# A 64-step recurrence scan with each head in its own 64-column tile, and its operands re-laid out in memory

## The chip, the cores and the metric

The kernel runs on one core of one Trainium2 chip. The metric is the device time of one execution in microseconds (us). Three runs of the kernel before gave 4600.29, 4602.82 and 4605.73 us; their median is 4602.82 us.

## What is computed

One transformer block on 512 tokens of width 2048: a projection of x by `w_in`, then two mixers side by side (stick-breaking attention and an RWKV7 time mix, 16 heads of 64 each), their gated sum, a layer norm, a mixture of 16384 rank-one experts, and a last layer norm. The change concerns the RWKV7 time mix:

```
def step(state, inp):                       # state: 16 heads of 64 x 64
    r_t, lw_t, k_t, v_t, a_t, b_t = inp
    sa = einsum('bhvk,bhk->bhv', state, a_t)
    state = (state * exp(lw_t)[:, :, None, :] + sa[..., None] * b_t[:, :, None, :]
             + v_t[..., None] * k_t[:, :, None, :])
    return state, einsum('bhvk,bhk->bhv', state, r_t)
```

Both kernels compute it in 8 chunks of 64 tokens (`NC = 8`, `L = 64`). Inside a chunk the recurrence is solved with a triangular 64 x 64 inverse for each head, so that a chunk is four matrix steps for each head: X (the state and the values seen through the rows a and k), U = inverse times X, S (the new state, from U, V and the decayed keys) and Y (the output). Only the state goes from one chunk to the next.

## The kernel before

The program is a row of stages with a barrier of all engines between them. Four of them matter here.

- `rwkv_prepare` (tensors `b_...`) goes over 8 blocks m of 128 channels (two heads, e = 0 and 1). Each block makes `ar` (rows a and r of all 8 chunks), `bk`, the masked products `gm` (in `b_wide`), the transposed keys `bkt` and the values `vt`, and SyncE (its queue is SPq in the rows) stores them to device memory for the scan: `stores(sp, m)`, lines 480 to 492, six DMAs a block. Beside this work TensorE multiplies pieces of late columns of `w_in` (class `Late`): GpSimd loads a piece (L323), ScalarE rounds it (L337), VectorE takes the rest (L344), TensorE multiplies (L102). SyncE also moves expert rows from memory to memory (`move_u`, L132), 16 DMAs of 128 KB a block.
- `attention_and_inverse` (tensors `d_...`) computes the attention and, on VectorE, the inverses (class `Inverse`, L752 loads the 128 triangular matrices, one a partition, L758 stores the result), with further late pieces beside it.
- `rwkv_scan` (tensors `s_...`) walks the 8 chunks. For each chunk SyncE loads `ar`, `g`, the lower half of `uv`, `wt` and `bkt` into one of two buffer sets (L825 to L829); a set is loaded again when the chunk that used it has ended on TensorE. TensorE then runs, strictly in this order: X (L858 and L862), U (L873), S (L882), Y (L889 and L893). In X and Y, one matmul for a pair of heads multiplies a block-diagonal 128 x 128 state, and one more for each head adds to it. All results of X, U and Y stand in PSUM partitions 0 to 63. VectorE and ScalarE copy half of X and half of U each (L932, L908, L934, L910), ScalarE copies Y (L914) and issues its store (L917). VectorE adds the old state to S (L938), waits until Y has read the old state, and multiplies by the decay (L944); the next chunk's X waits for that.
- `finish_and_mix` (tensors `m_...`) reads `y_d`; its first instructions (L1300, L1317) start behind the barrier.

A float32 matmul stands in the profile as two MATMUL and two LDWEIGHTS records. The order of the work is written out in the code; engines go through it in order and wait for semaphores.

## Time and profile before

| | us |
|---|---|
| median of three runs | 4602.82 |
| the profiled execution, its own time | 4599.9 |
| span of its trace, first to last instruction | 4598.0 |
| PE / VectorE / ScalarE / GpSimd busy | 4244.3 / 3204.7 / 1555.4 / 733.2 |
| mean granted TensorE clock, share of full speed | 0.968 |

The span and the time differ by 1.9 us, which lie before the first and after the last instruction. TensorE is busy for 92% of the span, but this is an average over stages: in the scan, from 1365.9 to 1487.8 us of the span, it is busy for 94.66 us of 121.9. Since every stage ends with a barrier, what a stage is worth is read inside it: which engine or queue ends last there.

### The profile page before, as it was taken

The numbers are of one execution on the slowest core, as the hardware profiler recorded it, in microseconds if no ns is written. First come the engines' busy times: TensorE is split into PE (matmuls) and PEld (weight loads), VectorE is DVE, ScalarE is ACT, GpSimd is POOL, SyncE is SP. The second block draws the span as 40 slices with busy tenths as digits, with TensorE's granted clock in tenths as the row PEclk, the third lists the DMA queues.
The fourth block names the chain that finished last, engine by engine and source line by source line (L and its number), as shares of the span: only waits on it lengthen the run. The fifth ranks groups of instructions, "written<-read, shape, count | busy, mean of one in ns | idle before, by whom it ended". The sixth has DMA issues, their size and how long they took to land. (4 is left out here: it accounts for less than half of the span.)

```text
span 4598.0 us, 61815 instructions
## 1 busy us (share of the span) xinstructions
PE 4244.3 (92%) x23132; PEld 3778.3 (82%) x23132; DVE 3204.7 (70%) x4942; ACT 1555.4 (34%) x2801; POOL 733.2 (16%) x629
## 2 busy tenths in 40 slices
PE   8999989979988899699977999999999999999994
PEld 6888865656767778587766999999999999999993
DVE  4444436746622644589447788899889999889996
ACT  2212113444431431222346333333333333333331
POOL 0000001123320000043620111111111111111110
PEclk9999999989999999799989999999999999999997
DMA  9999976776635559736537999999999999999994
GB/s 276 318 310 311 315 218 192 236 196 188 183 112 179 203 164 298 232 119 199 174 108 204 312 322 315 323 317 311 316 312 319 319 318 315 317 313 316 319 309 174
DMA packets 575824, 1182.01 MB, mean 257 GB/s; under 512 B 63432, under 2 KB 327472, under 8 KB 520784
## 3 DMA queue, kind: packets, MB, share of 16 engines
q1 hardware_dynamic: 505408, 809.48, 57.3%
q0 software_dynamic: 53120, 358.64, 21.7%
q10 hardware_dynamic: 17040, 10.49, 0.8%
q8 instruction: 159, 2.61, 0.2%
q14 instruction: 97, 0.79, 0.1%
HBM read 1009.00 MB, written 228.15 MB: 269 GB/s over the span
## 5 line engine op out<-in xcount | busy, mean ns | idle before, releaser
L102 PE MATMUL h_ps<-h_a,h_v 128*128 128x352 f32 x6144 | 1080.7, 324 | 23.1 <-DVE h_a L96 13.2
L102 PE MATMUL h_ps<-xs,h_ut 128*128 128x352 f32 x6144 | 1078.2, 324 | 16.9 <-DVE h_ut L96 16.9
L102 PEld LDWEIGHTS h_ps<-h_a,h_v 128*128 128x128 f32 x6144 | 1005.5, 189 | 31.9 <-DVE h_a L96 18.3
L102 PEld LDWEIGHTS h_ps<-xs,h_ut 128*128 128x128 f32 x6144 | 1010.6, 188 | 17.7 <-DVE h_ut L96 17.7
L102 PE MATMUL a_ps<-xt_hi,a_w 128*128 128x512 f32 x1792 | 553.9, 390 | 7.5 <-DVE a_w L96 7.5
L96 DVE TENSOR_TENSOR h_v<-h_v_raw,h_v 128x512 fp32r<-128x512 f32 x512 | 351.4, 686 | 83.4 <-ACT h_v L95 82.1
L102 PEld LDWEIGHTS a_ps<-xt_hi,a_w 128*128 128x128 f32 x1792 | 337.7, 188 | 77.9 <-issue 7.7
L95 ACT ACTIVATE h_v<-h_v_raw 128x512 fp32r<-128x512 f32 x512 | 319.0, 624 | 228.7 <-PE h_ps L102 226.7
L102 PE MATMUL a_ps<-xt_lo,a_w 128*128 128x512 f32 x896 | 349.5, 390 | 0.0
L2653 DVE SCALAR_TENSOR_TENSOR y_first<-h_rows,h_acts,y_first 128x2048 f32<-128x2048 f32 x128 | 300.4, 2347 | 0.0
L2647 DVE CUSTOM_DVE_ANT_0 h_rows<-h_rows,h_x_first 128x2048 f32<-128x2048 f32 x128 | 292.8, 2287 | 0.0
L96 DVE TENSOR_TENSOR h_ut<-h_u_raw,h_ut 128x512 fp32r<-128x512 f32 x288 | 198.5, 690 | 110.6 <-ACT h_ut L95 110.6
L2700 POOL DMA_INDIRECT h_rows<-in_peer_v,idx_first x128 | 139.4, 1089 | 687.7 <-DVE y_first L2653 474.2
L96 DVE TENSOR_TENSOR a_w<-a_raw,a_w 128x2048 fp32r<-128x2048 f32 x56 | 127.1, 2273 | 151.6 <-ACT a_w L95 79.6
L95 ACT ACTIVATE h_ut<-h_u_raw 128x512 fp32r<-128x512 f32 x288 | 179.3, 623 | 137.8 <-PE h_ps L102 100.7
L2700 POOL DMA_INDIRECT h_rows<-in_peer_u,idx_first x128 | 123.9, 968 | 631.1 <-DVE h_acts L2647 618.3
L95 ACT ACTIVATE h_a<-yt_last 128x352 fp32r<-128x352 f32 x128 | 64.0, 500 | 417.7 <-DVE yt_last L2621 413.4
L2637 DVE TENSOR_TENSOR yt<-yt,h_ps 128x352 f32<-128x352 f32 x403 | 202.7, 503 | 0.0
L102 PEld LDWEIGHTS a_ps<-xt_lo,a_w 128*128 128x128 f32 x896 | 168.9, 189 | 35.0
L96 POOL TENSOR_TENSOR f_w<-f_raw,f_w 128x2048 fp32r<-128x2048 f32 (+1 forms) x36 | 157.5, 4376 | 215.4 <-ACT f_w L95 215.4
L102 PE MATMUL b_ps<-xt_hi,b_half 128*128 128x512 f32 x512 | 179.8, 421 | 9.7 <-DVE b_half L344 9.6
L2568 ACT ACTIVATE h_acts<-h_acts 128x1 f32<-128x1 f32 x160 | 31.9, 199 | 457.6 <-DVE h_acts L2647 457.6
(355 smaller groups left out, 6699.9 us busy)
## 6 DMA issues: line engine op xcount, KB each, us to landing
h_v_raw<-in_peer_v SPq DMA_DIRECT2D x128, 1024.0 KB
h_u_raw<-turned_d SPq DMA_DIRECT2D x144, 512.0 KB
a_raw<-in_w_in SPq DMA_DIRECT2D x28, 2048.0 KB, 12.4
a_xin<-in_peer_u SPq DMA_DIRECT2D x224, 256.0 KB, 7.4
turned_d<-a_xin SPq DMA_DIRECT2D x56, 1024.0 KB, 6.5
raw_d<-in_peer_u SPq DMA_DIRECT2D x448, 128.0 KB, 4.3
h_u_raw<-raw_d SPq DMA_DIRECT2D x112, 512.0 KB
yt_last<-sums_d SPq DMA_DIRECT2D x124, 176.0 KB, 3.9
```

The lines of the kernel that those rows point to most:

```text
L95: return act.activation(hi, whole, ACT.Copy).then_inc(done, 1)
L96: return dve.tensor_tensor(lo, whole, hi.bitcast(F32), ALU.subtract).then_inc(done, 1)
L102: mm = pe.matmul(out, lhs[a], rhs[b], start=(first and n == 0), stop=(last and n == 2))
L2568: act.activation(acts[:, j:j + 1], acts[:, j:j + 1], ACT.Gelu).then_inc(dot_gelu, 1)
L2637: dve.tensor_tensor(out, out, made, ALU.add).then_inc(y_added, 1)
L2647: dve.tensor_tensor_reduce(rows[r % RR][:, :], rows[r % RR][:, :], x1[few][:, :], 1.0, 0.0, ALU.mult, ALU.add, acts[:, j:j + 1]).then_inc( ...
L2653: dve.scalar_tensor_tensor(y[:, :], rows[r % RR][:, :], acts[:, j:j + 1], y[:, :], ALU.mult, ALU.add).then_inc(row_used, 1)
L2700: pool.indirect_dma_start(rows[r % RR][:, :], None, u_rows if of_u else v_rows, bass.IndirectOffsetOnAxis(ap=fetch_idx[few][:, c:c + 1], a ...
```

## The change

- The scan holds each head alone. Head e of a pair has its own 64 partitions of PSUM and, where a product sums over 64 rows, its own 64 rows of the array. A product is one matmul for each head: the state (64 rows) and the values (the other 64 rows) stand in one 128-row operand `vk`, so that X and the first part of Y need one matmul where three stood. The old state enters S through a matmul with an identity that stands beside the keys (`vk[..., 1, ...]`). Only the first matmul in each bank and tile carries the flag that starts an accumulation.
- Y is computed in two parts: that of the state and values before U, that of `us` at the end. VectorE makes the next state with one multiply in four pieces (2 halves by 2 heads) into the next chunk's `vk`.
- There are four buffer sets in place of two. Loads are in two groups: `xg` and `vk` (X waits for these), `wt` and `gb` (U waits for these). SyncE issues the stores of y too. The loops of hardware (`Fori`) are gone.
- `rwkv_prepare` stores in the new layouts, 16 DMAs a block in place of 6, in runs of 256 and 512 bytes in place of 512 and 1024.
- The inverse is loaded and stored in one DMA each, 16 KB for each partition, in place of 8 each in runs of 256 bytes; the scan's load of `wt` (L851) takes runs of 256 bytes in place of rows of 4 KB. The store of y goes in runs of 256 bytes in place of rows of 4 KB.

```diff
-            sp.dma_start(ar_d[:, :, m].rearrange("c p j -> p c j"), ar[:, :, :, :].rearrange("p c a l -> p c (a l)"))\
-              .then_inc(s["st_ar"], 16)
+            for e in range(2):
+                q = slice(64 * e, 64 * e + 64)
+                sp.dma_start(xg_d[:, q, m, e].rearrange("c p j -> p c j"),
+                             ar[q, :, :, :].rearrange("p c a l -> p c (a l)")).then_inc(s["st_ar"], 16)
             sp.dma_start(bonus_d[m], bon[:, :]).then_inc(s["st_bon"], 16)
             sp.wait_ge(s["dve"], dv_.at(m, "masked3"))
-            sp.dma_start(g_d[:, :, 2 * m:2 * m + 2, :].rearrange("c p e j -> p c (e j)"),
-                         gm.rearrange("p c e j -> p c (e j)")).then_inc(s["st_gm"], 16)
+            for e in range(2):
+                rest = slice(64 - 64 * e, 128 - 64 * e)
+                q = slice(64 * e, 64 * e + 64)
+                sp.dma_start(gx_d.rearrange("(c e m) s t -> e m s c t", e=2, m=MB)[e, m], gm[0:64, :, e, 0:L])\
+                  .then_inc(s["st_gm"], 16)
+                sp.dma_start(gb_d[:, q, 0, m].rearrange("c s t -> s c t"), gm[0:64, :, e, L:2 * L])\
+                  .then_inc(s["st_gm"], 16)
+                sp.dma_start(xg_d[:, rest, m, e].rearrange("c s j -> s c j"), gm[64:128, :, e, :])\
+                  .then_inc(s["st_gm"], 16)
             sp.wait_ge(s["act"], ac_.at(m, "v_copied"))
-            sp.dma_start(bk_t_d[:, :, m].rearrange("c p j -> p c j"), bkt).then_inc(s["st_bkt"], 16)
-            sp.dma_start(v_d[:, :, m].rearrange("c p j -> p c j"), vt[:, :, :]).then_inc(s["st_vt"], 16)
+            for e in range(2):
+                q, rest, k = (slice(64 * z, 64 * z + 64) for z in (e, 1 - e, e))
+                sp.dma_start(gb_d[:, q, 1, m].rearrange("c s k -> s c k"), bkt[0:64, :, k]).then_inc(s["st_bkt"], 16)
+                sp.dma_start(vk_d[:, rest, 1, m].rearrange("c s k -> s c k"), bkt[64:128, :, k]).then_inc(s["st_bkt"], 16)
+                sp.dma_start(vk_d[:, rest, 0, m].rearrange("c s j -> s c j"), vt[:, :, k]).then_inc(s["st_vt"], 16)
...
     def load(self, queue):
-        for c in range(NC):
-            queue.dma_start(self.at[H * c:H * c + H, :, :], self.g_d[c, 0:L, :, 0:L].rearrange("s h t -> h s t"))\
-              .then_inc(self.a_in, 16)
+        queue.dma_start(self.at[:, :, :], self.gx_d).then_inc(self.a_in, 16)
 
     def store(self, sp):
         sp.wait_ge(self.row, 2 * L)
-        for c in range(NC):
-            sp.dma_start(self.wt_d[c].rearrange("j h t -> h j t"), self.wt[H * c:H * c + H, :, :])\
-              .then_inc(self.stored, 16)
+        sp.dma_start(self.wt_d, self.wt[:, :, :]).then_inc(self.stored, 16)
...
-        ar = [sb(f"ar{u}", [P, MB, 2 * L]) for u in range(2)]
-        bkt = [sb(f"bkt{u}", [P, MB, P]) for u in range(2)]
-        g = [sb(f"g{u}", [P, H, 2 * L]) for u in range(2)]
-        wt = [sb(f"wt{u}", [L, H, L]) for u in range(2)]
-        uv = [sb(f"uv{u}", [P, H, HD]) for u in range(2)]
-        xs = sb("xs", [L, H, HD])
-        ys = [sb(f"ys{u}", [L, H * HD]) for u in range(2)]
-        state = sb("state", [P, MB, P])
-        hsum = sb("hsum", [P, MB, HD])
+        xg = [sb(f"xg{u}", [P, MB, 2, 2 * L]) for u in range(R)]
+        gb = [sb(f"gb{u}", [P, 2, MB, HD]) for u in range(R)]
+        vk = [sb(f"vk{u}", [P, 2, 2, MB, HD]) for u in range(R)]
+        wt = [sb(f"wt{u}", [P, MB, L]) for u in range(R)]
+        xs, us = sb("xs", [P, MB, HD]), sb("us", [P, MB, HD])
+        ys = [sb(f"ys{u}", [P, MB, HD]) for u in range(2)]
+        ident = sb("ident", [P, P])
...
+        X, U, S = (ps[:, 2 * n:2 * n + 2, 0:T // 2].rearrange("p h (m j) -> p h m j", j=HD) for n in range(3))
+        Y = ps[:, 6, :].rearrange("p (m j) -> p m j", j=HD)
...
+            def load(c):
+                u = c % R
+                if c >= R:
+                    sp.wait_ge(pe_.sem, pe_.at(c - R, "y"))
+                sp.dma_start(xg[u][:, :, :, :], xg_d[c]).then_inc(x_in[u], 16)
+                for e in range(2):
+                    sp.dma_start(vk[u][rows(1 - e), e], vk_d[c, rows(1 - e)]).then_inc(x_in[u], 16)
+                for e in range(2):
+                    sp.dma_start(wt[u][rows(e), :, :], wv[c, e]).then_inc(rest_in[u], 16)
+                sp.dma_start(gb[u][:, :, :, :], gb_d[c]).then_inc(rest_in[u], 16)
+            load(0)
...
+            for c in range(1, R):
+                load(c)
+            for c in range(NC):
+                sp.wait_ge(ac_.sem, ac_.at(c, "y"))
+                for e in range(2):
+                    sp.dma_start(yv[c, e], ys[c % 2][rows(e), :, :]).then_inc(y_out[c % 2], 16)
+                if c + R < NC:
+                    load(c + R)
...
+            def each(ms, one):
+                for m in ms:
+                    for e in range(2):
+                        mm = one(m, e)
+                return mm
+
+            for c in range(NC):
+                u = c % R
+                pe.wait_ge(x_in[u], 48 * (c // R + 1))
+                for half in range(2):
+                    if c == 0:
+                        pe.wait_ge(zeroed, 2)
+                    else:
+                        pe.wait_ge(dv_.sem, dv_.at(c - 1, f"state{half}1"))
+                    each(heads(half), lambda m, e: pe.matmul(
+                        X[rows(e), m // MH, m % MH, :], xg[u][:, m, e, 0:L], vk[u][:, e, 0, m, :], start=True, stop=True))\
+                        .then_inc(pe_.sem, 1)
+                if c >= 1:
+                    pe.wait_ge(ac_.sem, ac_.at(c - 1, "y"))
+                each(range(MB), lambda m, e: pe.matmul(
+                    Y[rows(e), m, :], xg[u][:, m, e, L:2 * L], vk[u][:, e, 0, m, :], start=m == 0, stop=False,
+                    skip_group_check=True))
+                pe.wait_ge(rest_in[u], 48 * (c // R + 1))
+                for half in range(2):
+                    if half == 0:
+                        pe.wait_ge(dv_.sem, dv_.at(c, "x0"))
+                    else:
+                        pe.wait_ge(ac_.sem, ac_.at(c, "x1"))
+                    each(heads(half), lambda m, e: pe.matmul(
+                        U[rows(e), m // MH, m % MH, :], wt[u][rows(e), m, :], xs[rows(e), m, :], start=True, stop=True))\
+                        .then_inc(pe_.sem, 1)
+                if c == 0:
+                    pe.wait_ge(kept, 2 * R)
+                each(range(MB), lambda m, e: pe.matmul(
+                    S[rows(e), m // MH, m % MH, :], vk[u][:, e, 1, m, :], vk[u][:, e, 0, m, :], start=m % MH == 0, stop=False,
+                    skip_group_check=True))
+                for half in range(2):
+                    if half == 0:
+                        pe.wait_ge(dv_.sem, dv_.at(c, "u0"))
+                    else:
+                        pe.wait_ge(ac_.sem, ac_.at(c, "u1"))
+                    each(heads(half), lambda m, e: pe.matmul(
+                        S[rows(e), m // MH, m % MH, :], gb[u][rows(e), 1, m, :], us[rows(e), m, :], start=False, stop=True,
+                        skip_group_check=True)).then_inc(pe_.sem, 1)
+                each(range(MB), lambda m, e: pe.matmul(
+                    Y[rows(e), m, :], gb[u][rows(e), 0, m, :], us[rows(e), m, :], start=False, stop=True,
+                    skip_group_check=True)).then_inc(pe_.sem, 1)
...
+                after = vk[(c + 1) % R]
+                for half in range(2):
+                    dve.wait_ge(pe_.sem, pe_.at(c, f"s{half}"))
+                    for e in range(2):
+                        t.mark(f"state{half}{e}", dve.tensor_tensor(
+                            after[rows(e), e, 0, part(half), :], S[rows(e), half, :, :],
+                            dec[rows(e), part(half), c:c + 1].broadcast_to([64, MH, HD]), ALU.mult))```

SyncE's queue in `rwkv_prepare`, before: the stores of one block, between the loads of the next block (`b_zin`) and the moves of expert rows (`raw_d`).

```order
L516 DMA b_zin<-proj_t 128x512 x3
L482 DMA gate_d<-b_gs 128x512
L484 DMA ar_d<-b_ar 128x8x128
L486 DMA bonus_d<-b_bon 128x512
L488 DMA g_d<-b_wide 128x8x256
L491 DMA bk_t_d<-b_wide 128x8x128
L492 DMA v_d<-b_vt 64x8x128
L132 DMA raw_d<-in_peer_u 128x1x256 x16
```

And of the change, at the same place:

```order
L486 DMA xg_d<-b_ar 64x8x128 x2
L488 DMA bonus_d<-b_bon 128x512
L493 DMA gx_d<-b_wide 64x8x64
L495 DMA gb_d<-b_wide 64x8x64
L497 DMA xg_d<-b_wide 64x8x128
L493 DMA gx_d<-b_wide 64x8x64
L495 DMA gb_d<-b_wide 64x8x64
L497 DMA xg_d<-b_wide 64x8x128
L502 DMA gb_d<-b_wide 64x8x64
L503 DMA vk_d<-b_wide 64x8x64
L504 DMA vk_d<-b_vt 64x8x64
L502 DMA gb_d<-b_wide 64x8x64
```

Two more follow (L503, L504), then the 16 moves: they stand behind 16 stores now, where they stood behind 6. The last figure of a row is the run in elements of 4 bytes.

TensorE in `rwkv_scan`, before: the end of X, then U, S and the start of Y of one chunk.

```order
L858 MATMUL s_ps<-s_state,s_ar 64x128
L862 MATMUL s_ps<-s_uv,s_g 64x64 x2
...
L873 MATMUL s_ps<-s_xs,s_wt 64x64 x8
...
L873 MATMUL s_ps<-s_xs,s_wt 64x64 x8
...
L882 MATMUL s_ps<-s_uv,s_bkt 128x128 x4
...
L882 MATMUL s_ps<-s_uv,s_bkt 128x128 x4
...
L889 MATMUL s_ps<-s_state,s_ar 64x128
L893 MATMUL s_ps<-s_uv,s_g 64x64 x2
```

And of the change, one whole chunk (X, the first part of Y, U, the kept part of S, the rest of S, the rest of Y):

```order
L882 MATMUL s_ps<-s_vk,s_xg 64x64 x16
L887 MATMUL s_ps<-s_vk,s_xg 64x64 x16
L896 MATMUL s_ps<-s_xs,s_wt 64x64 x16
L901 MATMUL s_ps<-s_vk 64x64 x16
L909 MATMUL s_ps<-s_us,s_gb 64x64 x16
L912 MATMUL s_ps<-s_us,s_gb 64x64 x16
```

Half of Y has moved to between X and U, and a chunk has 96 matmuls of 64 columns where it had 48 of 64 and 24 of 128.

SyncE's queue at the start of `rwkv_scan`, of the change:

```order
L847 DMA s_xg<-xg_d 128x2048
L849 DMA s_vk<-vk_d 64x1024 x2
L851 DMA s_wt<-wt_d 64x8x64 x2
L852 DMA s_gb<-gb_d 128x1024
...
L860 DMA y_d<-s_ys 512x1x64 x2
L847 DMA s_xg<-xg_d 128x2048
```

Four chunks' loads stand ahead of the first store of y (L860); before, two chunks' loads stood in this queue and the stores of y in ScalarE's.

## Rows read from the trace of the kernel before

**Rows 1.** Busy time of each engine by stretch of the scan; columns stand in the first row.

```profile
core 0: us, PE busy (x) PEld busy (x) DVE busy (x) ACT busy (x) POOL busy (x), PEclk, DMA share, GB/s
...
1366.00:1376.70 10.70, 0.00 (x0) 0.00 (x0) 0.91 (x1) 0.00 (x0) 1.77 (x2) 0.50 0.89 290
1376.70:1381.20 4.50, 4.49 (x31) 4.50 (x32) 0.68 (x1) 0.00 (x0) 0.00 (x0) 0.50 1.04 351
...
1404.00:1484.00 80.00, 69.40 (x864) 67.03 (x864) 25.11 (x37) 14.20 (x25) 4.53 (x5) 1.00 0.58 184
```

**Rows 2.** Timeline of one chunk: start us, us, engine, line, operation, [idle before <-releaser].

```profile
1392.08 0.43 PE L858 MATMUL s_ps<-s_state,s_ar 128*64 128x128 f32 x2 [1.69 <-DVE s_state L944]
...
1395.84 2.08 PE L873 MATMUL s_ps<-s_xs,s_wt 64*64 64x64 f32 x32
...
1397.84 2.05 PE L882 MATMUL s_ps<-s_uv,s_bkt 128*128 128x128 f32 x16
...
1403.89 1.40 DVE L944 TENSOR_TENSOR s_state<-s_hsum,s_dec 64x512 f32<-64x512 f32 x2 [2.56 <-PE s_ps L893]
...
1405.35 0.43 PE L858 MATMUL s_ps<-s_state,s_ar 128*64 128x128 f32 x2 [1.70 <-DVE s_state L944]
```

**Rows 3.** Timeline of TensorE where row tiles, whole arrays and column tiles work.

```profile
983.09 1.16 PE L555 MATMUL b_ps<-b_ar,b_bk 64*128 64x128 f32 x16
984.18 1.09 PE L585 MATMUL b_ps<-b_ident,b_bk 128*128 128x128 f32 x8
...
4540.04 0.67 PE L2761 MATMUL r_ps<-r_ident,yt_last 128*32 128x128 f32 x12
```

**Rows 4.** DMA queues, 1367 to 1376 us (packets, MB, share); an issue with its landing us.

```profile
q1 hardware_dynamic: 737, 2.80, 97.8%
...
s_bkt<-bk_t_d SPq DMA_DIRECT2D x6, 512.0 KB, 8.4
```

**Rows 5.** The same view: 1307 to 1318, 988.5 to 996, and 1002 to 1032 us.

```profile
q1 hardware_dynamic: 5751, 1.74, 80.8%
...
q1 hardware_dynamic: 2574, 1.82, 83.1%
...
q0 software_dynamic: 640, 2.10, 65.9%
```

**Rows 6.** One block of `rwkv_prepare`: stretch, DMA queues, SyncE's moves, waits of 8 blocks.

```profile
888.00:922.00 34.00, 29.87 (x144) 20.79 (x142) 24.07 (x33) 15.26 (x23) 7.20 (x10) 1.00 0.79 244
...
q1 hardware_dynamic: 6529, 5.62, 51.3%
q0 software_dynamic: 800, 2.62, 27.3%
...
888.61 13.40 SPq L132 DMA_DIRECT2D raw_d<-in_peer_u  x16
...
ACT b_half L337 <- DMA b_raw<-in_w_in: 66.2, 22, 7.8
```

**Rows 7.** SyncE's timeline from the last masked product to the next stage.

```profile
988.61 0.37 SPq L488 DMA_DIRECT2D g_d<-b_wide  x1
...
992.67 1.20 SPq L523 DMA_DIRECT2D cols_d<-b_col  x1
...
999.89 1.29 SPq L1014 DMA_DIRECT2D d_qkv<-proj_t  x3
```

**Rows 8.** Start of the attention stage: a wait for a late piece, TensorE's, and ten us.

```profile
1032.90 0.63 ACT L337 ACTIVATE d_half<-d_raw 128x512 fp32r<-128x512 f32 x1 [9.59 <-DMA d_raw<-in_w_in]
...
1042.63 0.50 PE L102 MATMUL d_ps<-xt_hi,d_half 128*128 128x512 f32 x1 [2.19 <-DVE d_half L344]
...
1040.00:1050.00 10.00, 7.19 (x22) 4.84 (x21) 9.59 (x19) 2.50 (x7) 0.75 (x1) 0.83 0.50 148
```

**Rows 9.** From the scan's last copy of y to the next stage.

```profile
1483.25 0.58 ACT L914 COPY s_ys<-s_ps 64x512 f32<-64x512 f32 x1 [1.23 <-PE s_ps L893]
...
1487.85 0.39 SPq L1300 DMA_DIRECT2D m_raw<-in_w_up_a  x1
```

More of the change, by code:

```diff
@@ L801, in rwkv_scan @@
+        gb = [sb(f"gb{u}", [P, 2, MB, HD]) for u in range(R)]
[4 more added lines that the diff above has]
+        ident = sb("ident", [P, P])
         dec = sb("dec", [P, MB, NC])
         ps = ctx.enter_context(nc.psum_tensor("s_ps", [P, 8, T], F32))
-        loaded = [sem(f"loaded{u}") for u in range(2)]
@@ L815, in rwkv_scan @@
-        X, U, Y, S = (bank_pair(n) for n in range(4))
+        MH = MB // 2
+        X, U, S = (ps[:, 2 * n:2 * n + 2, 0:T // 2].rearrange("p h (m j) -> p h m j", j=HD) for n in range(3))
+        Y = ps[:, 6, :].rearrange("p (m j) -> p m j", j=HD)
+        x_in, rest_in = ([sem(f"{n}{u}") for u in range(R)] for n in ("x_in", "rest_in"))
+        const, dec_in, zeroed, kept = sem("const"), sem("dec_in"), sem("zeroed"), sem("kept")
+        y_out = [sem(f"y_out{u}") for u in range(2)]
+        pe_ = Steps(sem("pe"), 0, "x0 x1 u0 u1 s0 s1 y")
@@ new lines, in rwkv_scan, with rows, heads, part @@
+        dv_ = Steps(sem("dve"), 0, "x0 u0 state00 state01 state10 state11")
+        ac_ = Steps(sem("act"), 0, "x1 u1 y")
+        yv = y_d.rearrange("(c l) (m e j) -> c e l m j", l=L, e=2, j=HD)
+        wv = wt_d.rearrange("(c e m) j t -> c e j m t", e=2, m=MB)
+        block = ctx.enter_context(nc.Block())
+        def rows(e):
+            return slice(64 * e, 64 * e + 64)
+        def heads(half):
+            return range(MH * half, MH * (half + 1))
+        def part(half):
+            return slice(MH * half, MH * (half + 1))
@@ L919, in _ @@
-            for u in range(2):
-                act.wait_ge(y_out[u], 16 * (NC // 2) + 16)
+            for c in range(NC):
+                t = Turn(act, ac_, c)
+                act.wait_ge(pe_.sem, pe_.at(c, "x1"))
+                t.mark("x1", act.copy(xs[:, part(1), :], X[:, 1, :, :]))
+                act.wait_ge(pe_.sem, pe_.at(c, "u1"))
+                t.mark("u1", act.copy(us[:, part(1), :], U[:, 1, :, :]))
+                act.wait_ge(pe_.sem, pe_.at(c, "y"))
+                if c >= 2:
+                    act.wait_ge(y_out[c % 2], 32 * (c // 2))
+                t.mark("y", act.copy(ys[c % 2][:, :, :], Y[:, :, :]))
@@ new lines, in _ @@
+            for e in range(2):
+                dve.memset(vk[0][rows(e), e, 0, :, :], 0.0).then_inc(zeroed, 1)
+            dve.wait_ge(const, 2)
+            for u in range(R):
+                for e in range(2):
+                    dve.tensor_copy(vk[u][rows(e), e, 1, :, :],
+                                    ident[rows(e), rows(e)].unsqueeze(1).broadcast_to([64, MB, HD])).then_inc(kept, 1)
+            dve.wait_ge(dec_in, 16)
+            for c in range(NC):
+                t = Turn(dve, dv_, c)
+                dve.wait_ge(pe_.sem, pe_.at(c, "x0"))
+                t.mark("x0", dve.tensor_copy(xs[:, part(0), :], X[:, 0, :, :]))
+                dve.wait_ge(pe_.sem, pe_.at(c, "u0"))
+                t.mark("u0", dve.tensor_copy(us[:, part(0), :], U[:, 0, :, :]))
+                after = vk[(c + 1) % R]
+                for half in range(2):
+                    dve.wait_ge(pe_.sem, pe_.at(c, f"s{half}"))
+                    for e in range(2):
+                        t.mark(f"state{half}{e}", dve.tensor_tensor(
+                            after[rows(e), e, 0, part(half), :], S[rows(e), half, :, :],
+                            dec[rows(e), part(half), c:c + 1].broadcast_to([64, MH, HD]), ALU.mult))
@@ L984, in attention_and_inverse @@
         RR, WR, Q = late.RR, late.WR, late.Q
-        inverse = Inverse(sb, sem, g_d, wt_d)
+        inverse = Inverse(sb, sem, gx_d, wt_d)
         const, scaled = sem("const"), sem("scaled")
```

158 lines of the change are left out of this document (24 added, 134 removed).

## The prediction, made before the changed kernel ran

> **What bounds the kernel now.** I read the timeline of the scan first, then its waits and stretches, then the DMA view of each stage that the change touches. In the scan TensorE sets the pace. A chunk takes 1405.35 - 1392.08 = 13.27 us [rows 2]: TensorE works nearly all of it and then stands 1.70 us until VectorE has multiplied the state (1.40 us). The reader is to see that only this wait, not the loads, stands between chunks: between 1404 and 1484 us the DMA engines are 58% busy and TensorE is busy 69.40 of 80 us at full granted clock [rows 1]. The loads show at the start alone: nothing runs on TensorE from 1366.0 to 1376.7 us, and its first 4.5 us go at a granted clock of 0.50, the 1.2 GHz level [rows 1]. The stage ends at 1487.85, 4.0 us after the last copy of y (1483.25 + 0.58) [rows 9]. In `rwkv_prepare` a block takes some 34.4 us with TensorE busy 29.9 of 34 and the DMA engines 79% busy [rows 6]; ScalarE waits 66.2 us in 8 blocks for late pieces, so there the DMA engines are felt. The end of that stage is SyncE's stores [rows 7].
>
> **The scan's matmuls.** Now 192 records of 64 columns a chunk. Each alone costs (2.08 - 0.22)/31 = 60 ns (U, two halves; a record takes 0.22) [rows 2]: 192 x 60 = 11.5 us, scarcely under today's 13.27. What can bring more is tiles side by side. Row tiles do it: 16 records of 128 columns start within 1.16 - 0.27 = 0.89 us, 59 ns each, where 8 on the whole array need (1.09 - 0.27)/7 = 117 ns [rows 3]. Column tiles of 32 do it too, three beside each other: (0.67 - 0.27)/11 = 36 ns a record [rows 3]. Column tiles of 64 columns appear nowhere. Bounds for a record are so 60 ns (no overlap) and 30 ns (half of it); I take 36, the fastest supply of records seen. TensorE's chunk is 192 x 0.036 = 7.0 us, bounds 5.8 and 11.5. VectorE's and ScalarE's work has cover: copies of x lie beside the first part of Y (1.2 us), copies of u beside the kept part of S. The state is four pieces of 256 columns, at most half of today's 1.40 us a pair; the last pair ends while the last part of Y still runs. The 1.70 us wait goes; late next is TensorE itself, or the loads.
>
> **The scan's DMAs.** This is the term that decides. Today's 2.62 MB a chunk need 2.62/0.319 = 8.2 us (2.80 MB in 9 us at 97.8% give 0.319 MB/us while busy) [rows 4], and the last load lands after 8.4. Now a chunk loads 2.36 MB. Of it 2.10 MB go in rows of 4 and 8 KB: 6.7 us at 0.312 MB/us. The inverse goes in 1024 runs of 256 bytes, which cost 0.808 x 11 x 16/5751 = 24.7 ns of an engine each [rows 5]: 1.6 us. The y of a chunk is 1024 such runs too: 1.6 us. Sum 9.9 us a chunk: more than TensorE's 7.0. The scan turns from TensorE to the DMA engines. Four buffer sets let them run without a pause. First data move at about 1368.4 (8.2 us ahead of 1376.6); 8 loads of 8.3 and 7 stores of 1.6 end at 1446.0. The last chunk's U, S and rest of Y are 128 records, 4.6 us. The store of y(0) stands in SyncE's queue behind four chunks' loads, and the copy of y(c) waits for the store of y(c-2), behind which TensorE's next Y waits: I add 2 us. A copy of y, 0.6, then 4.0 + 0.8 for two DMAs in short runs: the next stage starts at 1458.0, 30 us earlier. If the runs were hidden among the long rows and TensorE set the pace, X could start at 1373 (1.57 MB, 5.0 us): 1373 + 8 x 7.0 + 2 (clock) + 1 + 4.8 = 1437, 51 us earlier. If tiles didn't overlap: 1373 + 8 x 11.5 + 2 + 5.4 = 1472, 15 us earlier.
>
> **`rwkv_prepare`.** Stores of a block are 2560 packets of 512 bytes and 1 KB, at 0.831 x 7.5 x 16/2574 = 38.7 ns, plus those of `ar`. Taking 30 ns for 512 bytes, between 24.7 and 38.7, today's are 6.2 + 1.9 = 8.1 us of all 16 engines. Now 5120 runs of 256 bytes and 2048 of 512: 7.9 + 3.8 = 11.7 us. So +3.6 us a block on 27 busy of 34.4. SyncE has ten issues more, some 5 us, beside 13.4 of moves and idle time for the rest. The moves come later and the late pieces meet more traffic. Bounds: 0 (all in gaps) and 3.6 x 8 = 29 us; I take 1 us a block, 8 us: ScalarE's waits are 8 us a block, but TensorE idles only 4.1 of 34 us for all reasons together [rows 6], so that about a quarter of the new traffic should reach it. The tail isn't hidden: after the last masked product the stores begin at 988.61, the last issue ends at 993.87, the next stage starts at 999.89 [rows 7]. In it 5120 + 1024 packets stand for 2560: 9.8 in place of 6.2 us, and nine more issues in front of the last: +5 us, bounds 3 and 9.
>
> **The attention stage.** Today the inverse's input takes 65.9% of 30 us, 19.8 us of all engines, for 2.10 MB [rows 5]. In long rows it is 6.6. That frees 13 us when late pieces wait 9.59 us; TensorE's stop of 2.19 us and the slow clock behind it (0.83 of 10 us, 1.7 us) may go [rows 8]: -4 us, bounds -7 and +1. The store of the inverse, 11 us of short runs, lies beside matmuls that don't wait for it: 0.
>
> **Sum.** -30 + 8 + 5 - 4 = -21 us against the profiled execution's own 4599.9: 4579. The median of the three runs is 2.9 above that execution; I predict 4580. A change of under 0.2%, 9 us, can't be told from none here.
>
> **Weighed against the skill.** The trace shows row tiles at 59 ns for 117 and column tiles only with 32 columns, whose weight loads are short [rows 3]. The Trainium skill, *TensorE: Matmul & The Clock Gate*, Packing small matmuls, says that a weight load overlaps running matmuls only when the row group differs; by this rule X, the first part of Y and the kept part of S would keep 60 ns and only the other half of the records fall to 30: 96 x 0.060 + 96 x 0.030 = 8.6 us a chunk, which is still under the 9.9 of the DMAs but rules out the fastest case. Column tiles here at 36 ns a record speak against it, without settling it. The skill, *DMA: Bandwidth & Descriptors*, Specifications, wants 512 bytes and more for line rate. The trace agrees: 256 bytes in 24.7 ns are 10 bytes a ns, where the scan's rows have 20 [rows 4, 5].
>
> **The rivals.**
> - TensorE sets the pace, the short runs cost nothing: -51 in the scan, +4 tail, 0 in the blocks, -4: 4549. For: DMA engines serve several queues at once. Against: 97.8% busy at 0.31 MB/us on long rows alone [rows 4].
> - The tiles don't run side by side (the change doesn't do what it says): -15 + 8 + 5 - 4 = -6: 4594. Against: [rows 3].
> - In between, TensorE falls to the 1.2 GHz level in waits for loads, as it did after a stop of 2.19 us [rows 8], though stops of 1.70 us left it at full [rows 1, 2]. A chunk then costs up to 2 us more than the DMAs' 9.9 in half of the chunks: 4587.
> - Slower than before: 256-byte runs between memory and SBUF cost what the inverse's input shows, 19.8 x 16/8192 = 38.6 ns [rows 5]. A block of `rwkv_prepare` then stores for 16.2 us in place of 8.1, the engines need 27 + 8.1 = 35.1 us a block, over its 34.4, and bursts come on top: +5 us a block, +40; tail +8; the scan's 2048 runs a chunk cost 1.8 more, so it saves 16. Sum +28: 4628. It decides from 3.5 us a block on. Against: 24.7 ns for the inverse's store, on SyncE's queue as here.
>
> **Numbers.** Forecast 0.55 (its own range 4566 to 4592), TensorE-paced 0.17, slow clock 0.08, tiles serial 0.11, slower 0.09. Faster by over 9 us: 0.53 + 0.17 + 0.06 + 0.05 = 0.81; within 9 us: 0.11; slower: 0.08. The range for 8 in 10 reaches to the first rival below and past the serial tiles above: 4547 to 4604.
>
> **What would show it.** Right: DMA share above 0.9 through the scan, TensorE idle some 3 us a chunk with a load of `s_gb` or `s_xg` as releaser, about 9.9 us a chunk, next stage 30 us earlier; a block of `rwkv_prepare` near 35.4; 5 us more from the last masked product to the attention stage; no wait of 9 us for the third late piece. Wrong: chunks of 7 us, or of over 11 with TensorE never idle; blocks of 38 us and more; records of L882, L887 and L901 not nearer than 58 ns.

## The result, and the profile after

| | before | changed |
|---|---|---|
| median | 4603.79 us (4 runs, 4600.29 to 4605.73) | 4571.74 us (4 runs, 4568.82 to 4579.62) |
| the profiled execution | 4599.9 us | 4569.34 us |
| span of its trace | 4598.0 us | 4567.8 us |

The ratio is 0.9936, 95% interval 0.9922 to 0.9949: 32 us faster. The forecast was 4580, with 4547 to 4604 as its range. The size of the largest term came out; what makes it did not, and two smaller terms missed in opposite directions. The first instruction of SyncE in each stage splits the span so:

| stage | before | changed | difference | predicted |
|---|---|---|---|---|
| up to the attention stage (`rwkv_prepare` with its tail) | 999.9 | 995.5 | -4.4 | +13 |
| attention and inverse | 366.1 | 362.7 | -3.3 | -4 |
| scan | 121.9 | 91.4 | -30.5 | -30 |
| all behind the scan | 3110.2 | 3118.2 | +8.0 | 0 |

SyncE in the scan of the changed kernel, where [rows 9] stood before (start us, us, engine, line, operation):

```profile
1358.24 0.33 SPq L847 DMA_DIRECT2D s_xg<-xg_d  x1
...
1445.63 1.19 SPq L860 DMA_DIRECT2D y_d<-s_ys  x2
1449.65 0.39 SPq L1305 DMA_DIRECT2D m_raw<-in_w_up_a  x1
```

Stretches of the scan, same columns as [rows 1]:

```profile
1376.00:1386.00 10.00, 5.63 (x128) 5.23 (x127) 2.11 (x5) 0.37 (x1) 0.00 (x0) 0.83 1.07 312
...
1406.00:1416.00 10.00, 7.27 (x140) 6.90 (x140) 2.19 (x6) 1.08 (x3) 0.00 (x0) 0.66 1.08 274
...
1436.00:1446.00 10.00, 8.97 (x280) 8.49 (x276) 4.22 (x10) 1.93 (x5) 0.00 (x0) 1.00 0.15 31
```

The DMA engines are full until about 1430 us, as forecast: their share, the time of all packets over that of 16 engines, is 1.07 and 1.08. TensorE is idle for 4.4 and 2.7 us of the 10 in the first two stretches. So far the forecast seems right. But what TensorE waits for is something else. Its waits from the second chunk on (engine, tile, line <- what ended the wait: us in total, times, longest):

```profile
PE s_ps L882 <- issue: 4.4, 2, 3.0
PE s_ps L909 <- issue: 3.4, 2, 2.7
PE s_ps L912 <- issue: 2.8, 1, 2.8
PE s_ps L896 <- issue: 2.7, 2, 2.2
PE s_ps L887 <- issue: 2.5, 1, 2.5
```

No load ends any of them. They meet five of the six products of a chunk; only L901, the kept part of S, is never met. "Issue" means that nothing the profile shows was awaited. The timeline of TensorE shows where they fall:

```profile
1377.93 1.98 PE L887 MATMUL s_ps<-s_vk,s_xg 128*64 128x64 f32 x32 [2.51 <-issue]
1379.84 1.56 PE L896 MATMUL s_ps<-s_xs,s_wt 64*64 64x64 f32 x32
1381.33 1.15 PE L901 MATMUL s_ps<-s_vk 128*64 128x64 f32 x32
1382.41 1.15 PE L909 MATMUL s_ps<-s_us,s_gb 64*64 64x64 f32 x32
1386.38 1.15 PE L912 MATMUL s_ps<-s_us,s_gb 64*64 64x64 f32 x32 [2.82 <-issue]
1387.46 1.88 PE L882 MATMUL s_ps<-s_vk,s_xg 128*64 128x64 f32 x32
1389.12 1.92 PE L887 MATMUL s_ps<-s_vk,s_xg 128*64 128x64 f32 x32
1390.98 1.15 PE L896 MATMUL s_ps<-s_xs,s_wt 64*64 64x64 f32 x31
1394.28 0.27 PE L896 MATMUL s_ps<-s_xs,s_wt 64*64 64x64 f32 x1 [2.16 <-issue]
```

Count the records between two stops: 32 + 32 + 32 + 32 = 128, then 32 + 32 + 32 + 31 = 127. Further on it is 127, 128, 254 (two portions, with no stop between them), 128 and 127. The stops come after equal portions of code, whatever the code does. The DMA queues of 1360 to 1430 us name the portion (packets, MB, share):

```profile
q1 hardware_dynamic: 16515, 19.72, 108.1%
q8 instruction: 8, 0.13, 0.9%
```

A packet of the instruction queue has 0.13 MB / 8 = 16 KB; 128 matmul and 128 weight load records are 256, so 64 bytes each. Between 1376 and 1446 us the changed kernel fetched 11 such packets, and the kernel before, whose TensorE ran the scan in a loop of two chunks, 2. Each of the eight stops ends 2.3 to 3.3 us after such a packet has begun to move: those that begin at 1375.5, 1383.8 and 1391.6 us belong to the stops that end at 1377.93, 1386.38 and 1394.28. The one of 1412.1 us meets no stop; it is the boundary inside the 254. The eight stops sum to 15.8 us. After most of them the records are slow: the 32 of L887 take 1.98 us at 1377.93 and 1.10 at full clock. The granted clock is 0.83 and 0.66 in the first two stretches above. From 1365.98 to 1445.0 TensorE's part lasts 79.0 us. Eight chunks at full clock and without a stop are 50.2 (6.27 each, measured below), the stops 15.8; the 13 us left are the slower records, those at the clock's lower level, in these stretches and at the start.

The theory to test (A): TensorE's code, written out, must be fetched in 16 KB pieces; behind full data queues a piece comes too late. The rivals: the loads themselves pace the scan (my forecast, D); TensorE's fetching is slow in any case.

### The profile page after: what moved, and what is told of

The parts are those of the page before. It is cut to its first block and busy times, and to the rows that moved or that the text cites. A ratio compares the mean times of both kernels' runs of the same rounds, so it can differ in the third digit from the quotient of the medians.

```text
span 4567.8 us, 62381 instructions
## 1 busy us (share of the span) xinstructions
PE 4207.3 (92%) x23516; PEld 3742.7 (82%) x23516; DVE 3196.5 (70%) x4951; ACT 1545.0 (34%) x2793; POOL 718.8 (16%) x616
## 5 line engine op out<-in xcount | busy, mean ns | idle before, releaser
L102 PE MATMUL h_ps<-h_a,h_v 128*128 128x352 f32 x6144 | 1079.4, 324 | 24.8 <-DVE h_a L96 13.5
L102 PE MATMUL h_ps<-xs,h_ut 128*128 128x352 f32 x6144 | 1079.4, 325 | 18.9 <-DVE h_ut L96 18.9
L102 PEld LDWEIGHTS h_ps<-h_a,h_v 128*128 128x128 f32 x6144 | 1004.4, 189 | 33.5 <-DVE h_a L96 18.7
L102 PEld LDWEIGHTS h_ps<-xs,h_ut 128*128 128x128 f32 x6144 | 1011.6, 189 | 19.8 <-DVE h_ut L96 19.7
L102 PE MATMUL a_ps<-xt_hi,a_w 128*128 128x512 f32 x1792 | 553.9, 390 | 7.5 <-DVE a_w L96 7.5
L102 PEld LDWEIGHTS a_ps<-xt_hi,a_w 128*128 128x128 f32 x1792 | 337.8, 188 | 77.9 <-issue 7.8
L102 PE MATMUL a_ps<-xt_lo,a_w 128*128 128x512 f32 x896 | 349.7, 390 | 0.0
L102 PEld LDWEIGHTS a_ps<-xt_lo,a_w 128*128 128x128 f32 x896 | 168.8, 188 | 35.0
L102 PE MATMUL b_ps<-xt_hi,b_half 128*128 128x512 f32 x512 | 176.8, 416 | 8.3 <-DVE b_half L344 8.3
## 6 DMA issues: line engine op xcount, KB each, us to landing
h_u_raw<-turned_d SPq DMA_DIRECT2D x144, 512.0 KB, 10.2
h_u_raw<-raw_d SPq DMA_DIRECT2D x112, 512.0 KB, 9.8
```

Of the source, the lines that this page charges most:

```text
L102: mm = pe.matmul(out, lhs[a], rhs[b], start=(first and n == 0), stop=(last and n == 2))
```

## The experiments

The stages of every kernel that ran, in us, by SyncE's first instruction in each stage of the profiled execution. The median of the kernel before was 4603.3 to 4605.4 us beside them. How far two profiles of one program lie apart is seen in the two rows of the changed kernel. The time up to the attention stage is not in the table: it is 995.5 to 1001.7 us in the eleven kernels from "changed" to "the same, loop", 997.8 on average, 998.5 with the short stores alone, and 999.9 and 1000.6 with the old stores. Of the 4.4 us above, some 2 are thus common to the kernels and the rest is this profile.

| kernel | median | attention | scan | behind it |
|---|---|---|---|---|
| before | 4603.8 | 366.1 | 121.9 | 3110.2 |
| changed | 4571.7 | 362.7 | 91.4 | 3118.2 |
| changed, again | 4572.1 | 364.6 | 90.5 | 3116.9 |
| tiles one after the other | 4582.0 | 361.9 | 97.2 | 3117.8 |
| two buffer sets | 4574.9 | 362.2 | 93.5 | 3118.0 |
| two sets, loop | 4569.6 | 363.9 | 92.8 | 3118.7 |
| no loads of chunks 4 to 7 | 4556.4 | 361.7 | 73.9 | 3121.0 |
| long rows in scan | 4573.6 | 362.0 | 91.1 | 3120.4 |
| inverse stored in 16 parts | 4581.5 | 371.8 | 90.7 | 3115.7 |
| the same, loop | 4569.3 | 371.0 | 88.0 | 3114.2 |
| inverse stored in 8 parts | 4574.1 | 362.2 | 87.3 | 3117.5 |
| the same, loop | 4561.6 | 362.5 | 90.4 | 3117.1 |
| before + short stores | 4603.7 | 368.1 | 120.9 | 3112.3 |
| before + inverse in one load | 4596.7 | 362.2 | 122.3 | 3110.5 |

**1. Take the data traffic away.**

```diff
-                if c + R < NC:
-                    load(c + R)
...
-                pe.wait_ge(x_in[u], 48 * (c // R + 1))
+                pe.wait_ge(x_in[u], 48)
...
```

> The changed kernel, but the loads of the scan's chunks 4 to 7 are left out (they compute on the operands of chunks 0 to 3). The DMA engines have nothing to do from about 1403 us on but the stores of y. Theory A (instruction fetches wait behind data): the stops every 128 records shrink from 1.4 to 3 us to 0.6 us or less once the loads end, the clock stays at full, chunks 4 to 7 take 6.3 to 7 us each in place of 9.2; scan 80 to 83 us, total 4560 to 4564. Rival (the stops belong to TensorE's own way of fetching, not to the DMA traffic): stops of 2 us and more stay to the end, scan above 87 us.

The wait on `rest_in` is changed in the same way. Measured: scan 73.9 us, 17.5 shorter, the median 4556.4 (ratio to before 0.9894, interval 0.9879 to 0.9909). TensorE's waits after its first product:

```profile
PE s_ps L910 <- issue: 3.7, 1, 3.7
PE s_ps L885 <- issue: 2.8, 1, 2.8
PE s_ps L894 <- issue: 1.6, 1, 1.6
```

The last of them ends at 1393.45, about when the loads end. After it the share of the DMA engines is 0.23:

```profile
1396.00:1406.00 10.00, 10.00 (x314) 9.58 (x312) 4.29 (x11) 2.29 (x5) 0.00 (x0) 1.00 0.23 50
```

TensorE's chunks follow each other without a hole, every one in 1409.29 - 1403.02 = 6.27 us:

```profile
1403.02 1.24 PE L880 MATMUL s_ps<-s_vk,s_xg 128*64 128x64 f32 x32
1404.09 1.10 PE L885 MATMUL s_ps<-s_vk,s_xg 128*64 128x64 f32 x32
1405.12 1.15 PE L894 MATMUL s_ps<-s_xs,s_wt 64*64 64x64 f32 x32
...
1409.29 0.89 PE L880 MATMUL s_ps<-s_vk,s_xg 128*64 128x64 f32 x20
```

The instruction packets are as many as before, 12 in the scan, and 9 of them move between 1394 and 1428 us, where TensorE doesn't stop once: they come in time now. This refutes the rival of a fetch that is slow in any case. It was more than A had expected (80 to 83): once the loads have ended the stops vanish altogether, and do not only shrink.

**2. Keep the traffic, take the fetches away.** First the control, two buffer sets, then the loop on it.

```diff
-    R = 4
+    R = 2
```

> The changed kernel with two buffer sets in the scan in place of four, TensorE's code still written out chunk by chunk. It is the control for the next one. Theory A (TensorE stops for its own instructions, every 128 records, behind the loads): the stops of 1.4 to 3 us with no releaser stay, the scan is 91 to 94 us. Rival (the depth of the prefetch was what the change needed): the loads of a chunk start only when the chunk two before has ended, TensorE waits 3 us and more a chunk for s_xg or s_gb, scan above 96 us.

```diff
-            for c in range(NC):
-                u = c % R
...
+            for c in range(2):
+                chunk(c, c - 1, c, 48, c == 0)
+            with pe.Fori(0, NC // 2 - 1) as i:
+                for u in range(2):
+                    chunk(i * 2 + (u + 2), i * 2 + (u + 1), u, i * 48 + 96, False)
```

The looped kernels here and in experiment 4 also raise a semaphore ahead of each product on TensorE; in their first pass they stop all the same, so this is not what takes the stops away.

> Two buffer sets, and TensorE's chunks 2 to 7 in a hardware loop of two chunks (768 instructions), so that its instructions need not be fetched again for chunks 4 to 7. Theory A (instruction supply behind saturated data queues stops TensorE): no stop without a releaser from chunk 4 on, clock at full there, chunks of 6.3 us plus what the loads ask; some wait for loads appears, since the DMA engines need 8.75 us a chunk; scan 80 to 86 us, total 4562 to 4568. Rival (the loads pace the scan at about 9.2 us a chunk in any case): the stops turn into waits for s_xg of the same length, scan within 3 us of that of the two written-out sets. Rival (a loop of 48 KB of instructions does not stay resident): stops as before, the same time.

Measured: 93.5 and 92.8 us of scan; medians 4574.9 (4570.8 to 4576.7) and 4569.6 (4565.9 to 4576.7). TensorE's waits for `s_vk` in the control, the 12.2 us before its first product among them, and then its waits in the looped one, from 1398 us on:

```profile
PE s_ps L882 <- DMA s_vk<-vk_d: 25.9, 6, 12.2
```

```profile
PE s_ps L883 <- DMA s_vk<-vk_d: 12.1, 4, 4.7
PE s_ps L914 <- issue: 2.0, 1, 2.0
PE s_ps L899 <- DMA s_gb<-gb_d: 1.1, 2, 0.6
```

The one stop left lies in the loop's first pass, at 1408.4 to 1410.4; from chunk 4 on there is none, and the instruction queue moved 6 packets between 1376 and 1446 us in place of 11. So the stops are fetches, as A says. But the scan is no shorter. With two sets a load can only start when the chunk two before has ended, and it takes the stops' place: 13.2 us of waiting for loads. The first rival of the expectation, not A, had the total right. The control has the same waits already (13.7 us for `s_vk`, after its first product) beside 6.1 us of stops, so its 93.5 us fit A's 91 to 94 by number alone. The loads bind here, since a chunk asks the DMA engines for 2.62 MB, some 9.3 us at the 19.72 MB in 70 us of the rows above.

**3. Is it the short runs?**

```diff
-        yv = y_d.rearrange("(c l) (m e j) -> c e l m j", l=L, e=2, j=HD)
-        wv = wt_d.rearrange("(c e m) j t -> c e j m t", e=2, m=MB)
+        yv = y_d.rearrange("(c l) w -> c (l w)", l=L).rearrange("c (e p f) -> c e p f", e=2, p=64)
+        wv = wt_d.rearrange("(c e m) j t -> c e (m j t)", e=2, m=MB).rearrange("c e (p f) -> c e p f", p=64)
...
```

> The changed kernel, but the scan loads the inverse and stores y in rows of 2 KB (the values go to other places of memory; this leaves the right order of both out). Theory D (my prediction: the short runs are 3.3 us of DMA time a chunk and the DMA engines pace the scan): the DMA time of a chunk falls from 9.9 to 6.9 us, the scan is 20 us shorter and more. Theory A (TensorE stops for its instructions behind saturated queues; the loads alone still saturate them): stops stay until the loads end, which is some 6 to 10 us earlier, scan 84 to 90 us.

Measured: scan 91.1 us, median 4573.6: no gain. The same 70 us of the queues:

```profile
q1 hardware_dynamic: 5804, 20.22, 99.0%
q8 instruction: 8, 0.13, 0.8%
```

A third of the packets moved 20.22 MB where 16515 had moved 19.72: 10700 packets fewer bring 2.5%, a little more if one counts that this stage began 1.4 us later. D would have had the scan over 20 us shorter. It also takes from A: the loads end earlier, as the same stretch shows in the changed kernel and then in this one (DMA share 0.75 and 0.32), but the scan doesn't:

```profile
1426.00:1436.00 10.00, 8.79 (x227) 8.13 (x225) 2.96 (x7) 1.68 (x4) 0.00 (x0) 0.87 0.75 150
```

```profile
1426.00:1436.00 10.00, 7.79 (x238) 7.39 (x237) 2.67 (x7) 1.71 (x4) 0.00 (x0) 1.00 0.32 92
```

TensorE still stops 7 times, up to 4.53 us, so a piece comes late behind full engines also where rows of 2 to 8 KB carry nearly all the bytes (share 0.99).

**4. Four sets, rows of 2 KB for the inverse, with and without a loop of four chunks.** The inverse is stored in runs of 256 bytes (beside attention's matmuls) and the scan loads rows of 2 KB. First with 16 stores of 8 partitions:

```diff
-        sp.dma_start(self.wt_d, self.wt[:, :, :]).then_inc(self.stored, 16)
+        for g in range(2 * NC):
+            sp.dma_start(self.wt_d[g].rearrange("j m t -> m j t"), self.wt[MB * g:MB * g + MB, :, :])\
+              .then_inc(self.stored, 16)
...
```

> The changed kernel, but the inverse is stored in 16 DMAs in runs of 256 bytes into the order of the scan, and the scan loads it in 64 rows of 2 KB a half. A chunk of the scan then asks 1024 packets of 256 bytes less of the DMA engines. Theory A (loads saturate the DMA engines, and TensorE's instruction fetches wait behind them): the loads end some 8 us earlier (7.5 in place of 8.75 us a chunk), the stops at the end of the scan vanish sooner, scan 83 to 88 us in place of 91.4; attention within 1 us, since the store lies beside matmuls. Total 4563 to 4568. Rival (the number of stops and their length per 128 records decide, whatever the loads ask): scan within 2 us of 91.4. Rival (the short runs only move and now delay the attention stage's late pieces): attention 3 us longer, total as the changed kernel.

> As the kernel with the inverse in long rows, and TensorE's scan in a hardware loop of four chunks run twice, with four buffer sets kept: instructions of chunks 4 to 7 are fetched already (98 KB in the loop), while the loads are four chunks ahead. Theory A: no stop without a releaser from chunk 4 on, clock at full there, chunks of 6.3 us unless a load is late; scan 77 to 83 us, total 4556 to 4564. Rival (98 KB of instructions do not stay resident): stops as in the written-out kernel, same time as it. Rival (the loads bind as soon as the stops are gone): the stops become waits for s_xg, scan within 2 us of the kernel with long rows alone.

Measured: both lose 8 to 9 us in the attention stage (371.8 and 371.0 us), where the stores keep SyncE for 26.6 to 27.8 us:

```profile
1301.01 27.76 SPq L768 DMA_DIRECT2D wt_d<-d_wt  x16
```

The third case of the first expectation, then, and larger than it said. Without the loop the scan did not gain (90.7). With it the stops end with the loop's first pass, at 1422.7; the last three chunks follow in 6.4 us each. Scan 88.0, where A had 77 to 83, since the five stops of the first pass alone take 16.9 us; median 12.2 us lower. The stores in 8 parts of 16 partitions, as the kernel before had them:

```diff
-        sp.dma_start(self.wt_d, self.wt[:, :, :]).then_inc(self.stored, 16)
+        for c in range(NC):
+            sp.dma_start(self.wt_d[c].rearrange("j h t -> h j t"), self.wt[H * c:H * c + H, :, :])\
+              .then_inc(self.stored, 16)
...
```

> The same without the loop: TensorE's chunks are written out. Theory A (stops for instructions stay as long as the loads saturate the DMA engines, and fewer loads do not shorten a stop): 7 or 8 stops of 1.9 to 3.7 us, scan 90 to 92 us, 3 us more than with the loop; attention 361 to 364; total 4566 to 4572. Rival (the lighter loads shorten the scan by themselves): scan 88 or less without the loop too.

> The inverse stored in 8 DMAs of 16 partitions (as the kernel before did, runs of 256 bytes) and loaded by the scan in rows of 2 KB; TensorE's scan in a loop of four chunks run twice. Against the version with 16 stores of 8 partitions, whose attention stage took 371 us: Theory A (the store's cost was its 27 us in SyncE's queue, in front of what attention loads and moves there): attention 361 to 364 us, scan 88 as there, total 4559 to 4564, the fastest. Rival (any store in runs of 256 bytes at this place costs attention 8 us): attention 370, total 4568 to 4572.

> The changed kernel unchanged, beside the next three on the same chip, and a second profile of it. Expected: 4570 to 4576, scan 91 to 93 us, rwkv_prepare 335 to 341 us (the spread of the profiles so far), out_project 235 to 238 us between its first product and that of the next stage (231 to 232 in the kernel before). If the second profile shows 231 to 232 there, the 4 us that this stage lost are chance; if 235 and more again, they belong to the change.

Measured: attention is back at 362 us in both, so the store's cost was that of the 16 parts, as A said. Written out 4574.1 us (4570.1 to 4577.7), looped 4561.6 (4557.2 to 4568.9), the changed kernel again 4572.1 (4570.5 to 4574.6). The looped one is the fastest kernel here that leaves nothing out, ratio to before 0.9903 (0.9888 to 0.9918), and its slowest run was faster than the fastest of the changed kernel beside it. Its waits after the first product:

```profile
PE s_ps L884 <- issue: 7.0, 2, 4.2
PE s_ps L913 <- issue: 6.6, 2, 3.6
PE s_ps L899 <- issue: 2.4, 1, 2.4
```

Five stops, all in the first pass (the last ends at 1416.64), and longer than in the changed kernel (3.2 us on average for 2.0). The three pairs written out and looped differ by 5.3, 12.2 and 12.5 us in their medians, but by 0.5, 6.1 and 1.4 in the spans of the profiled executions. The looped kernel's profile is of its slowest run, with a scan of 90.4 us: it doesn't show where the others gain 10 us, and that stays open. In the profiles the written-out kernel has the shorter scan, 87.3 us with seven stops of 15.3 us. That is within the 88 of its expectation's rival, not the 90 to 92 of A, but 90.7 us was measured for the same scan in the version with 16 stores, so one profile doesn't decide it. Nor do the profiles show that the loop saves time in the stops: there are fewer, and their sum, 16.0 us, is that of the changed kernel. That the looped version is faster rests on the medians alone.

**5. The tiles.**

```diff
-                for m in ms:
-                    for e in range(2):
+                for e in range(2):
+                    for m in ms:
```

> The changed kernel, but TensorE walks all pairs of one head side (e = 0) and then those of the other, so that neighbouring matmuls are in the same tile. Theory A (two 64-column tiles run side by side when they alternate, about 34 ns a record while warm): now 58 to 60 ns a record, 32 records of U in some 2.0 us at full clock, a chunk at least 192 x 0.059 = 11.3 us, the scan 15 to 22 us longer than the 91.4 of the changed kernel, total 4587 to 4594. Rival (the loads pace the scan, tiles do not matter): a chunk 10 to 11.3 us, scan at most 10 us longer. Rival (tiles did not overlap in the change either): same time as the changed kernel within 3 us.

Measured: scan 97.2 us, median 4582.0 (4574.1 to 4585.8). A chunk at full clock takes 1440.87 - 1431.62 = 9.25 us, where alternating tiles take 6.27; 32 records of L901 take 1.90 us and those of L896 1.54 (timeline, and then a stretch of TensorE):

```profile
1431.62 1.37 PE L882 MATMUL s_ps<-s_vk,s_xg 128*64 128x64 f32 x29
...
1434.60 1.54 PE L896 MATMUL s_ps<-s_xs,s_wt 64*64 64x64 f32 x32
1436.06 1.90 PE L901 MATMUL s_ps<-s_vk 128*64 128x64 f32 x32
...
1440.87 1.37 PE L882 MATMUL s_ps<-s_vk,s_xg 128*64 128x64 f32 x29
```

```profile
1406.00:1416.00 10.00, 9.95 (x200) 9.40 (x198) 2.54 (x6) 1.33 (x3) 0.00 (x0) 1.00 1.10 271
```

That is (1.90 - 0.22)/31 = 54 ns a record for (1.15 - 0.22)/31 = 30 in L901, whose products stay in one tile for 16 records; L896 changes tile every 8 records and takes 43 ns. A had taken 59 for all, and so 11.3 us a chunk. The tiles run side by side in the change. Yet of 8 x 3.0 = 24 us only 5.8 show in the stage. TensorE asks for 16 KB of code every 6.2 us in place of 4.2, the stops shrink to four of 1.0 to 1.8 us, 5.4 in all, and the granted clock stays at 1.00 from 1396 us on. 74.0 + 5.4 of stops + 5.5 of slow clock is its 84.9 us. Neither A's 15 to 22 nor the rivals said this; it is what A implies, had I worked it through.

**6. `rwkv_prepare` alone:** the kernel before with the stores split as in the change.

```diff
-            sp.dma_start(bk_t_d[:, :, m].rearrange("c p j -> p c j"), bkt).then_inc(s["st_bkt"], 16)
-            sp.dma_start(v_d[:, :, m].rearrange("c p j -> p c j"), vt[:, :, :]).then_inc(s["st_vt"], 16)
+            for e in range(2):
+                k = slice(64 * e, 64 * e + 64)
+                sp.dma_start(bk_t_d[:, 0:64, m, k].rearrange("c s k -> s c k"), bkt[0:64, :, k]).then_inc(s["st_bkt"], 16)
+                sp.dma_start(bk_t_d[:, 64:128, m, k].rearrange("c s k -> s c k"), bkt[64:128, :, k]).then_inc(s["st_bkt"], 16)
+                sp.dma_start(v_d[:, :, m, k].rearrange("c s j -> s c j"), vt[:, :, k]).then_inc(s["st_vt"], 16)
...
```

> The kernel before with one part of the change alone: the stores of rwkv_prepare are split as in the change (16 DMAs a block, runs of 256 and 512 bytes), into the old tensors, so that scan and attention stay as they were. My prediction priced this part at +13 us (8 in the blocks, 5 in the tail). Theory P (as predicted): the stage and the total are 8 to 13 us longer than before. Theory Q (from the two traces: the blocks of the changed kernel are 6.7 us shorter in all, its tail 2.2 longer): the stores cost nothing in the blocks or even less, because they delay SyncE's moves of expert rows away from the late pieces; stage -5 to 0, total -5 to +3. Rival: the shorter blocks of the changed kernel are not from the stores at all (run-to-run phase of the moves); then the stage here is within 2 us of before plus 2 for the tail.

Measured: ratio 1.0006, interval 0.9997 to 1.0015, so +2.8 us with -1.4 to +6.9 as its bounds. Theory P is refuted. Q fits, and so does the rival: the stage ends 1.4 us sooner than before. From the first block's last masked product to the eighth's it takes 235.8 us, against 238.9 and 240.1 in the two profiles with the old stores, and 232.2 to 239.3 in the eleven other profiles with the new ones; from there to the next stage 14.3 us for 12.0. The traffic did grow (720 to 990 us, the kernel before and then the changed one):

```profile
q1 hardware_dynamic: 47758, 40.81, 47.7%
```

```profile
q1 hardware_dynamic: 77517, 41.83, 57.4%
```

57.4 less 47.7%, 9.7% of 270 us, are 26 us in these eight blocks, near the 3.6 a block of the forecast. It all lay beside other work. Whether the stores make the blocks shorter isn't shown, since 235.8 lies only 3.1 under the nearer of the two old profiles and the new ones spread over 7. If they do, why is open: the moves of expert rows begin 7 to 8 us later in a block and are issued faster (one burst 10.81 us for 13.40 in [rows 6]), but no run moved them alone.

**7. The inverse's load alone:**

```diff
-        for c in range(NC):
-            queue.dma_start(self.at[H * c:H * c + H, :, :], self.g_d[c, 0:L, :, 0:L].rearrange("s h t -> h s t"))\
-              .then_inc(self.a_in, 16)
+        queue.dma_start(self.at[:, :, :].rearrange("p s t -> p (s t)"),
+                        self.u_d.rearrange("o (p s) d -> p (o s d)", s=2)[0:P]).then_inc(self.a_in, 16)
...
```

> The kernel before, but the inverse's input comes in one DMA of 16 KB rows, from another tensor of the same size (so its values are other numbers; this leaves the true input out). The prediction: the third late piece no longer waits 9.59 us, TensorE's stop of 2.19 us and the slow clock behind it go, the attention stage is 4 us shorter (bounds 7 shorter and 1 longer). Rival: the 3.3 us that the stage lost in the changed kernel came from elsewhere (the order in which the stage starts after a different prepare stage), and here it stays within 1 us of 366.

Measured: attention 362.2 us, 3.8 shorter; total ratio 0.9985 (0.9975 to 0.9994). The software queue from 1002 to 1032 us, and the late piece of [rows 8]:

```profile
q0 software_dynamic: 144, 2.10, 17.2%
```

```profile
1027.79 0.63 ACT L337 ACTIVATE d_half<-d_raw 128x512 fp32r<-128x512 f32 x1 [3.46 <-DMA d_raw<-in_w_in]
```

5.2 us of all engines for 19.8, and 3.46 us of waiting for 9.59: the forecast's step as it stood, and TensorE's stop of 2.19 us is gone.

## Why the prediction was right or wrong

- **The scan, -30: the size right, the mechanism wrong.** The step that failed is "late next is TensorE itself, or the loads", and with it "TensorE idle some 3 us a chunk with a load as releaser". The third candidate, TensorE's own code, was in the change's description in so many words (the loops are gone) and in the order of instructions, and I gave it no price. Experiment 1 shows that the loads cause the stops, and experiment 3 that the scan doesn't end sooner when the loads do. The term was met by luck as far as its working goes: the loads ask for 9.3 us a chunk (I had 9.9), and stops and slow clock bring TensorE's 6.3 us to a like pace (stores of y(2) to y(4) start 9.2 us apart). Why the two paces lie together, and what the stops alone cost while the loads go on, no run shows: with two sets the loads took the stops' place. The rival of a slow clock, given 0.08, had a part of it: TensorE did fall to the lower level, behind stops for code and not for loads, and 13 of its 79 us are that. Chunks near 7 us, named as a sign that the forecast is wrong, appeared at the end, where the loads were done.
- **TensorE's chunk, 7.0 us:** 6.27, 30 to 34 ns a record where I took 36 from a column tile of 32. The bounds held. The rule of the Trainium skill (*TensorE: Matmul & The Clock Gate*, Packing small matmuls), by which a weight load overlaps only another row group, would keep X, the first part of Y and the kept part of S, which use all 128 rows, at serial speed; the measurement decides otherwise, 30 ns alternating and 54 in series for L901. The 60 ns that I took for a tile by itself were 43 to 54 in experiment 5.
- **The short runs in the scan, 3.3 us a chunk:** experiment 3 finds none in the time. The 24.7 ns of [rows 5] were read where short runs stood alone; among long rows they raise the share (1.08 for 0.99) and hardly cost throughput. The Trainium skill, *DMA: Bandwidth & Descriptors*, Specifications, wants 512 bytes for line rate; the stretch of short runs alone agrees (10 bytes a ns), but in this mix they cost 2.5%.
- **`rwkv_prepare`, +8 and +5:** measured -3.1 and +2.3 alone, -6.7 and +2.2 in the changed kernel. The DMA time was right; the step that failed is "a quarter of the new traffic should reach TensorE". Its lower end, all in gaps, was the case; a gain, which I had excluded, was excluded by no row, and no run settles whether there is one. In the tail, the stores are issued over 11 us and land meanwhile: SyncE then waits 2.4 us where it had waited 6.0.
- **Attention, -4:** -3.3, and -3.8 alone.
- **What the sum did not hold:** +8 us behind the scan. It is in every kernel with the new scan (3114.2 to 3121.0 us) and in none with the old one (3110.2, 3110.5, 3112.3), so a loss is hardly chance, though its size ranges from 2 to 11 us. A good part lies in `out_project`, 236.4 us from its first product to the next stage's for 231.7; run again it was 234.6, between the 232 that I had called chance and the 235 that I had called the change's: VectorE waits 22.1 us for the residual `in_x` where it waited 19.6, and TensorE then stops 3.24 us. Nothing in the stage was changed; what moved its loads stays open.
- **The sum:** 17 us too much in `rwkv_prepare`, 8 too little behind the scan, and so 4580 for 4572.

## What to carry to other kernels

Where a change writes out a loop or cuts matmuls into smaller ones, count the bytes of code that TensorE runs through per microsecond, and look at what fills the DMA engines meanwhile; the loops here stopped for it in their first pass only. In a timeline, stops "<- issue" at equal counts of records, and not at a wait in the program, were such fetches here; the queue "instruction" of the DMA view is where to check it. An engine that gets faster asks for its code faster: of the 24 us that alternating tiles save TensorE here, 18 were given back in stops and in the slow clock behind them.
